# The routed experts of an encoder layer: results added to the residual in memory, per step

## The chip, the core and the metric

The kernel runs on one core of one Trainium2 chip. The metric is the device time of one execution in microseconds (us); three runs of the kernel before gave 1376.01, 1379.69 and 1382.04, median 1379.69. A core has a matrix engine (TensorE, PE in the profile, with its weight loads as PEld), VectorE (DVE), ScalarE (ACT), GpSimd (POOL) and SyncE (SP), each with an instruction stream of its own that runs in order, and 16 DMA engines that all of them feed. SP and POOL issue the transfers here. What SP issues goes over the hardware queue (q1 in the profile), what POOL issues over the software queue (q0).

## The reference

One encoder layer over 1296 positions (16 shared meta tokens, and two sequences of 1024 and 256): a mixer of windowed attention and a recurrence, then a mixture of 32 experts, then a final norm. The change lies in the expert part:

```python
def hier_moe(u, p):                       # u: [1280 tokens + meta, 1024], float32
    grp = argmax(u @ w_router_grp + b)    # one of 4 groups
    top_v, top_i = top_k(in_group_logits, 2)
    gates = softmax(top_v) * p_grp
    eid = grp * 8 + top_i                 # two experts for each token
    # for every expert e over its tokens xb, in blocks:
    #   hid = silu(xb @ w_g[e]) * (xb @ w_u[e]);  y = hid @ w_d[e]
    # out[token] += gate * y
h = h + hier_moe(rmsnorm(h), p)
return rmsnorm(h, ln_final_g)[:, N_META:]
```

An expert has three matrices of 512 x 1024 float32, 2 MB each. 1280 tokens go to two experts each, 2560 rows in all.

## The kernel before

The program has five stages that follow each other, each closed by a barrier of all engines: `project` and `keys` (projections, recurrence), `mix` (attention, output product, router), `plan`, `experts` and `combine`. For each block of 128 tokens, `mix` writes the residual to `h2_dram` and its norm to `u_dram`, and with two indirect DMAs the token numbers into `list_dram`, which has a list of 1280 places for every expert. `plan` reads the counts and makes with 27 small VectorE operations a table of steps: one step is up to 128 tokens of one expert. This input gives 35 steps over 32 experts.

`experts` (line 1681) does the steps. A float32 product is made of three products of rounded parts: every matrix and every activation is split into a high part (ACT copies it, rounding to the PE's format) and a low part (DVE subtracts). Weights come in chunks of 1 MB, 128 x 2048, six for an expert (two each of gate, up, down: G, U, D), into six slots `raw`, each with its `e_hi` and `e_lo`. A repeated expert's chunks are neither loaded nor split again.

- SP (`step`, lines 1789 to 1812) issues per step n one list (`ix`, 128 token numbers), and then the chunks D of step n, U of n+1 and G of n+2, each when DVE has done with the slot before. At the start it holds all but one chunk back until the first gather has landed.
- POOL (lines 1829 to 1868) gathers the 128 rows of `u_dram` that a list names into `ex` (two buffers; `gather(n + 3)` or so, two to three steps ahead), and stores the 128 x 1024 result of a step to consecutive rows of `y_dram` (`store`, L1847).
- PE (`step`, line 1914): turn x of step n+1 (8 transposes), up product of n (24 matmuls), first half of the gate product of n+1 (12), turn the hidden values of n (4 transposes), second half of that gate product (12), down product of n (24).
- ACT (`step`, line 1973): silu of n, high part of x of n+1, `y_from_psum` of the step before (L1970), and the high parts of six chunks with the high part of the hidden values among them. DVE makes the low parts and the product silu times up in the same order.
- At the start of `experts`, DVE computes for each token the rows of `y_dram` where its two results will stand (`slots`, lines 2053 to 2059).

`combine` (line 2075) then gathers, on POOL, 2 x 10 tiles of 128 rows from `y_dram` (L2115), adds each times its gate to the residual (L2142), norms and stores. Five of the ten residual tiles are loaded at the end of `experts`.

Of the kernel before, what the change touches and what calls it, by code (L numbers as in the profile page):

```python
# [69 lines left out]
FIELDS = 6  # L70
MAXPAIRS = (2 * REAL // P + EXP) // 2
YROWS = 2 * REAL + P
ROUT = 40

DEPTH = 5
# [28 lines left out]
def encoder(nc, a, out):  # L104
    top = ExitStack()
    with top:
# [6 lines left out]
        h2_dram = dram("h2_dram", [REAL, D], F32)  # L113
        u_dram = dram("u_dram", [REAL, D], F32)
        k_dram = dram("k_dram", [P, 2, 2, META + P + REAL + P], F32R)
        y_dram = dram("y_dram", [YROWS, D], F32)
        list_dram = dram("list_dram", [(EXP + 1) * LIST, 1], I32)
        table_dram = dram("table_dram", [MAXBLK, FIELDS], I32)

# [6 lines left out]
        expert1 = keep("expert1", [P, NB])  # L126
        expert2 = keep("expert2", [P, NB])
        place1 = keep("place1", [P, NB])
        place2 = keep("place2", [P, NB])
# [5 lines left out]
        with ExitStack() as mixer:  # L135
# [7 lines left out]
            with semaphores(nc) as own:  # L143
                project(nc, own, a, feat, k_pre, v_pre, ident, eps_t, iota_e, list_dram, y_dram)
# [11 lines left out]
                gate1, gate2, expert1, expert2, place1, place2, counts, h2_dram, u_dram, list_dram)  # L156
        slots = [top.enter_context(nc.sbuf_tensor(f"slot{j}", [P, NB], I32)) for j in range(2)]
        start = keep("start", [P, EXP])
        table = top.enter_context(nc.sbuf_tensor("table", [1, MAXBLK * FIELDS], I32))
        plan(nc, sem, counts, start, table, table_dram)  # L160

        z = [keep(f"z{s}", [P, D]) for s in range(DEPTH)]
        g_final = keep("g_final", [P, D])
        z_in = [sem(f"z_in{s}") for s in range(DEPTH)]
        g_in = sem("g_in")
        experts(nc, sem, a, ident, iota_e, start, expert1, expert2, place1, place2, slots, table, list_dram,
                u_dram, h2_dram, y_dram, g_final, z, g_in, z_in)
        combine(nc, sem, eps_t, gate1, gate2, slots, h2_dram, y_dram, out, g_final, z, g_in, z_in)


def project(nc, sem, a, feat, k_pre, v_pre, ident, eps_t, iota_e, list_dram, y_dram):
# [8 lines left out]
    with ExitStack() as ctx:  # L180
# [20 lines left out]
        zeros = a_g[:, 0:D]  # L201
        conv = h_g[:, :]
# [21 lines left out]
        fills = sem("fills")  # L224
        fill_dma = sem("fill_dma")
# [52 lines left out]
        def _(sp):  # L278
# [11 lines left out]
            for f in range(2):  # L290
# [3 lines left out]
            sp.wait_ge(fills, 2)  # L294
            sp.dma_start(list_dram.rearrange("(p c) o -> p (c o)", p=P),
                         zeros[:, 0:(EXP + 1) * LIST // P].bitcast(I32)).then_inc(fill_dma, 16)
            sp.dma_start(y_dram[2 * REAL:YROWS, :], zeros).then_inc(fill_dma, 16)
# [21 lines left out]
        @block.gpsimd  # L319
        def _(pool):  # L320
            pool.memset(zeros, 0.0).then_inc(fills, 1)
            pool.iota(iota_e[:, :], pattern=[[1, EXP]], base=0, channel_multiplier=0,
                      allow_small_or_imprecise_dtypes=True).then_inc(fills, 1)
            pool.memset(xr[:, :, :], 0.0).then_inc(xr_cleared, 1)

        @block.scalar
        def _(act):
# [86 lines left out]
            act.wait_ge(fill_dma, 32)  # L414
# [40 lines left out]
        def _(dve):  # L455
# [29 lines left out]

            dve.wait_ge(consts_in, 32)
# [322 lines left out]
def mix(nc, sem, a, spare, q_pre, rec, rstd_rec, w_hi, w_lo, k_dram, v_tok, v_meta, ident, eps_t, iota_e,  # L809
        gate1, gate2, expert1, expert2, place1, place2, counts, h2_dram, u_dram, list_dram):  # L810
# [6 lines left out]
    with ExitStack() as ctx:  # L817
# [68 lines left out]
        token_s = [sb(f"token_s{s}", [P, 1], I32) for s in range(RING)]  # L886
# [177 lines left out]
        def _(pool):  # L1064
# [41 lines left out]
            def place(b, s):  # L1106
# [4 lines left out]
                pool.tensor_copy(token_s[s][:, :], token[:, bass.ds(b, 1)]).then_inc(token_done, 1)  # L1111
                pool.wait_ge(token_done, b + 1)
                take_waits(pool)
                for j in range(2):
                    pool.indirect_dma_start(list_dram, bass.IndirectOffsetOnAxis(ap=addr[j][s][:, 0:1], axis=0),
                                            token_s[s][:, 0:1], None).then_inc(listed[s], 16)
# [461 lines left out]
PLAN_STEPS = 27  # L1578


def plan(nc, sem, counts, start, table, table_dram):

    with ExitStack() as ctx:
# [7 lines left out]
        count_end = sb("count_end", [P, EXP])  # L1597
# [5 lines left out]
        n_tokens = sb("n_tokens", [P, 1])  # L1603
        offset = sb("offset", [P, 1])
        row = sb("row", [P, FIELDS])
        row_i = sb("row_i", [P, FIELDS], I32)
        n_less_1 = sb("n_less_1", [P, 1])
        n_experts_1 = sb("n_experts_1", [P, 1])
        pairs_i = sb("pairs_i", [P, 1], I32)
# [8 lines left out]
        def _(pool):  # L1618
# [3 lines left out]
            pool.iota(n_less_1[:, :], pattern=[[0, 1]], base=-1, channel_multiplier=1,  # L1622
                      allow_small_or_imprecise_dtypes=True).then_inc(set_up, 1)

        @block.vector
        def _(dve):
# [8 lines left out]
            dve.wait_ge(set_up, 3)  # L1635
# [3 lines left out]
            then(dve.tensor_copy(blocks[:, :], blocks_i[:, :]))  # L1639
            then(dve.tensor_tensor_scan(block_end[:, :], ones[:, :], blocks[:, :], 0.0, ALU.mult, ALU.add))  # L1640
            then(dve.tensor_tensor_scan(count_end[:, :], ones[:, :], counts[:, :], 0.0, ALU.mult, ALU.add))
            then(dve.tensor_tensor(start[:, :], count_end[:, :], counts[:, :], ALU.subtract))
            then(dve.tensor_scalar(before_n[:, :], block_end[:, :], n_col[:, 0:1], None, ALU.is_le))
            then(dve.tensor_reduce(n_experts[:, :], before_n[:, :], AX.X, ALU.add))
            for total, each in ((n_blocks, blocks), (n_tokens, counts)):
                then(dve.tensor_tensor(weighed[:, :], before_n[:, :], each[:, :], ALU.mult))
                then(dve.tensor_reduce(total[:, :], weighed[:, :], AX.X, ALU.add))

            then(dve.tensor_tensor(offset[:, :], n_col[:, :], n_blocks[:, :], ALU.subtract))
            then(dve.tensor_scalar(offset[:, :], offset[:, :], float(P), None, ALU.mult))  # L1650
            then(dve.tensor_scalar(row[:, 0:1], n_experts[:, :], float(EXP - 1), None, ALU.min))

            then(dve.tensor_scalar(before_n[:, :], block_end[:, :], n_less_1[:, 0:1], None, ALU.is_le))
            then(dve.tensor_reduce(n_experts_1[:, :], before_n[:, :], AX.X, ALU.add))
            then(dve.scalar_tensor_tensor(out=n_experts_1[:, :], in0=n_less_1[:, :], scalar=0.0, in1=n_experts_1[:, :],
                                          op0=ALU.min, op1=ALU.add))
            then(dve.tensor_scalar(row[:, 3:4], n_experts_1[:, :], row[:, 0:1], None, ALU.is_lt))
            then(dve.scalar_tensor_tensor(out=row[:, 1:2], in0=n_experts[:, :], scalar=float(LIST), in1=offset[:, :],
                                          op0=ALU.mult, op1=ALU.add))
            then(dve.tensor_tensor(row[:, 2:3], n_tokens[:, :], offset[:, :], ALU.add))  # L1660

            then(dve.tensor_scalar(pairs_i[:, :], block_end[:, EXP - 1:EXP], -2.0, None, ALU.add))
            then(dve.tensor_single_scalar(pairs_i[:, :], pairs_i[:, :], 1, ALU.arith_shift_right))
            then(dve.tensor_copy(row_i[:, 0:4], row[:, 0:4]))
            then(dve.tensor_copy(row_i[:, 4:5], pairs_i[:, :]))
            then(dve.scalar_tensor_tensor(out=n_blocks[:, :], in0=pairs_i[:, :], scalar=-2.0, in1=block_end[:, EXP - 1:EXP],
                                          op0=ALU.mult, op1=ALU.add))
            then(dve.tensor_scalar(row_i[:, 5:6], n_blocks[:, :], -2.0, None, ALU.add))
# [10 lines left out]


def experts(nc, sem, a, ident, iota_e, start, expert1, expert2, place1, place2, slots, table, list_dram,
            u_dram, h2_dram, y_dram, g_final, z, g_in, z_in):

    with ExitStack() as ctx:
# [83 lines left out]
        def _(sp):  # L1775
# [11 lines left out]
            for m in range(2):  # L1787
                lists(m, m)
# [446 lines left out]
```

## Time and profile before

| what | value |
|---|---|
| runs | 1376.01, 1379.69, 1382.04 us |
| profiled execution | 1379.8 us, span of its instructions 1377.9 us |
| mean granted PE clock | 0.937 of full speed |
| PE busy | 1204.5 us (87%) |
| DVE, ACT, POOL busy | 921.3 (67%), 846.8 (61%), 196.7 (14%) us |
| HBM read, written | 274.21 MB, 37.96 MB |
| stages | to the plan 638 us, plan and start of the experts to 662 us (first gate product), steps to 1312 us, combine to the end |

The profiled execution took 1.9 us more than its span. Times in the rows count from the start of the span. A share of 1.00 of the DMA engines in a stretch means that the sum of the time of their packets was 16 times the stretch; packets of two queues can overlap in an engine, so it can pass 1. The matmuls overlap each other in the record: one follows the other after 0.23 us though each has 0.39.

### The profile page before, as it was taken

Reading aid. Unit: us, or ns where it says so; the run is one execution under the profiler, and the core shown is the slowest. Engines: PE = TensorE matmul, PEld = TensorE weight load, DVE = VectorE, ACT = ScalarE, POOL = GpSimd, SP = SyncE. Lnnn points to the kernel's source line nnn. Section 1 sums busy time; section 2 is a strip of 40 time slices with the busy share of each in tenths; the row PEclk is TensorE's granted clock in tenths of the full one; section 3 lists DMA queues with packets and bytes.
Section 4 is the critical chain, followed back from the end, with each engine's and each line's share of the span. In section 5 each row is a group of like instructions: output and inputs, shape, how many; then the busy total and the mean of one; then the engine's idle time right before and its main releaser. Section 6 shows DMA issues by size and latency. Waiting matters only on the chain. (4 is left out here: it accounts for less than half of the span.)

```text
span 1377.9 us, 22574 instructions
## 1 busy us (share of the span) xinstructions
PE 1204.5 (87%) x5971; PEld 1012.3 (73%) x5971; DVE 921.3 (67%) x1175; ACT 846.8 (61%) x1013; POOL 196.7 (14%) x201
## 2 busy tenths in 40 slices
PE   4999999847999999980799999999999999999900
PEld 3998888845788888860688888888888888888800
DVE  5575555244566766643788876665888888988638
ACT  6438888254666566630687765555777777778412
POOL 1000000031122322111011111101111011112041
PEclk9999999957999999985799999999999999999965
DMA  5210110093232343110999987678999999999758
GB/s 182 88 52 25 38 38 15 11 299 106 82 81 81 110 124 88 46 62 15 396 420 418 419 324 299 266 280 325 383 394 406 398 408 403 396 403 407 261 201 347
DMA packets 74905, 313.35 MB, mean 227 GB/s; under 512 B 15329, under 2 KB 26210, under 8 KB 50290
## 3 DMA queue, kind: packets, MB, share of 16 engines
q1 hardware_dynamic: 54450, 256.71, 48.5%
q0 software_dynamic: 20416, 56.18, 11.6%
q8 instruction: 17, 0.28, 0.1%
q14 instruction: 22, 0.18, 0.0%
HBM read 274.21 MB, written 37.96 MB: 227 GB/s over the span
## 5 line engine op out<-in xcount | busy, mean ns | idle before, releaser
L2011 DVE TENSOR_TENSOR e_lo<-raw,e_hi 128x2048 fp32r<-128x2048 f32 x192 | 432.5, 2287 | 68.8 <-ACT e_hi L1949 63.6
L1949 ACT ACTIVATE e_hi<-raw 128x2048 fp32r<-128x2048 f32 x192 | 356.1, 1912 | 59.3 <-DMA raw<-in_w_gate 39.7
L603 PE MATMUL pj<-h_hi,w_hi 128*128 128x432 f32 x336 | 123.5, 368 | 0.0
L1883 PE MATMUL ps_g<-e_hi,ex_hi 128*128 128x512 f32 x288 | 118.2, 410 | 4.1 <-DVE ex_lo L2026 4.1
L603 PE MATMUL pj<-h_lo,w_hi 128*128 128x432 f32 x336 | 121.0, 360 | 0.0
L603 PE MATMUL pj<-h_hi,w_lo 128*128 128x432 f32 x336 | 120.5, 358 | 0.0
L1883 PE MATMUL ps_g<-e_hi,ex_lo 128*128 128x512 f32 x288 | 115.0, 399 | 0.0
L1883 PE MATMUL ps_g<-e_lo,ex_hi 128*128 128x512 f32 x288 | 114.8, 399 | 0.0
L1883 PE MATMUL ps_u<-e_hi,ex_hi 128*128 128x512 f32 x280 | 113.8, 407 | 0.0
L1838 POOL DMA_INDIRECT ex<-u_dram,ix x37 | 67.9, 1836 | 319.3 <-DMA ix<-list_dram 318.9
L1883 PE MATMUL ps_u<-e_lo,ex_hi 128*128 128x512 f32 x280 | 110.8, 396 | 0.0
L1883 PE MATMUL ps_u<-e_hi,ex_lo 128*128 128x512 f32 x280 | 110.6, 395 | 0.0
L1908 PE MATMUL ps_ey<-e_hi,hid_lo 128*128 128x512 f32 x280 | 110.5, 395 | 0.0
L1908 PE MATMUL ps_ey<-e_hi,hid_hi 128*128 128x512 f32 x280 | 110.3, 394 | 0.0
L1908 PE MATMUL ps_ey<-e_lo,hid_hi 128*128 128x512 f32 x280 | 110.3, 394 | 0.0
L1965 ACT ACTIVATE ex_hi<-ps_ex 128x1024 fp32r<-128x1024 f32 x36 | 36.9, 1026 | 92.1 <-PE ps_ex L1875 92.1
L1410 DVE CUSTOM_DVE_ANT_0 probs<-ps_sc,mask,sink_bc 128x400 f32<-128x400 f32 x80 | 47.7, 631 | 41.8 <-PE ps_sc L1145 41.7
L1883 PEld LDWEIGHTS ps_g<-e_hi,ex_hi 128*128 128x128 f32 x288 | 55.1, 191 | 16.7 <-DVE ex_lo L2026 2.8
L1875 PE MATMUL ps_ex<-ident,ex 128*128 128x128 f32 x288 | 40.8, 286 | 30.2 <-DMA ex<-u_dram,ix 30.2
L603 PEld LDWEIGHTS pj<-h_hi,w_hi 128*128 128x128 f32 x336 | 63.5, 189 | 3.3
L603 PEld LDWEIGHTS pj<-h_lo,w_hi 128*128 128x128 f32 x336 | 63.7, 190 | 2.8
L603 PEld LDWEIGHTS pj<-h_hi,w_lo 128*128 128x128 f32 x336 | 63.5, 189 | 2.9
(276 smaller groups left out, 2354.8 us busy)
## 6 DMA issues: line engine op xcount, KB each, us to landing
raw<-in_w_gate SPq DMA_DIRECT2D x64, 1024.0 KB, 10.0
raw<-in_w_up SPq DMA_DIRECT2D x64, 1024.0 KB, 8.1
raw<-in_w_down SPq DMA_DIRECT2D x64, 1024.0 KB
y_dram<-y_sb POOLq DMA_DIRECT2D x35, 512.0 KB
k_win<-k_dram POOLq DMA_DIRECT2D x20, 384.0 KB, 7.3
w_raw<-in_w_in SPq DMA_DIRECT2D x14, 512.0 KB, 3.7
xh<-in_x SPq DMA_DIRECT2D x10, 512.0 KB, 6.5
h_dram<-xh SPq DMA_DIRECT2D x10, 512.0 KB, 2.8
```

Of the source, the lines that this page charges most:

```text
L603: mm = pe.matmul(ps[:, bank, 0:CH], w[s][:, k, :], h[:, k, cols], start=(k == 0 and n == 0), stop=(k == KD - 1 and n == 2))
L1410: dve.tensor_tensor_reduce(probs[:, h, :], ps_sc[h % 2][:, 0:KEYS], mask[s][:, :], HD ** -0.5, sink[:, h:h + 1], ALU.add, ALU.max, smax[:, ...
L1838: pool.indirect_dma_start(x[s][:, :], None, u_dram, bass.IndirectOffsetOnAxis(ap=ix[s][:, 0:1], axis=0)).then_inc(x_in[s], 16)
L1875: mm = pe.transpose(ps_x[:, c, k * P:(k + 1) * P], x[s][:, c * FE + k:(c + 1) * FE:KG], ident[:, :])
L1883: mm = pe.matmul(ps[:, :], xs[s][:, c * KG + k, :], w[slot][:, k * FE:(k + 1) * FE], start=(c == 0 and k == 0 and n == 0), stop=(c == 1 an ...
L1908: mm = pe.matmul(ps_y[:, i, :], h[:, c * KDN + k, :], w[D0 + c][:, k * D + i * BANK:k * D + (i + 1) * BANK], start=(c == 0 and k == 0 and ...
L1949: act.activation(w_hi[s][:, :], raw[s][:, :], ACT.Copy).then_inc(hi_done, 1)
L1965: act.activation(x_hi[s][:, :, :], square_x(ps_x), ACT.Copy).then_inc(x_hi_done, 1)
L2011: dve.tensor_tensor(w_lo[s][:, :], raw[s][:, :], w_hi[s][:, :].bitcast(F32), ALU.subtract).then_inc(lo_done, 1)
```

## The change

`combine` is gone. What it did is spread out:

- The lists. An entry of `list_dram` is now a pair, token number and gate. `mix` writes both (four small copies on POOL for a block of tokens in place of one). Unused entries name a row past the tokens, 1280 plus the entry's number modulo 128, so the 128 rows that a step names are all different; `h2_dram` and `u_dram` have 128 more rows for them, filled with zeros. Before, an unused entry named token 0.
- The plan has 18 operations in place of 27, gives every expert at least one step, and knows therefore that step 0 is expert 0. The slot operations at the start of `experts` are gone.
- The end of a step. ACT multiplies the result by the gates as it copies it out of PSUM, and POOL adds the tile to `h2_dram` with an indirect DMA that accumulates (`add_to_h2`, L1822 of the new file). Adds of two steps may name the same token, so the list of the next step's rows is only read, and `y_listed` only raised, when the add before has landed; `y_from_psum` waits for `y_listed`.
- The queues. POOL issues the two lists of a step (`ix_x` for the gather, `ix_y` for the add), SP only weights. x, its list and its split parts have one buffer in place of two. `gather(m)` is issued after x of step m-1 has been turned and, by POOL's order, after the list of y of step m-3 has landed.
- The order of PE: gate product of n+1, turn hidden of n, up of n+1, turn x of n+2, down of n. There is no gate product of a 36th step any more (before, the last step made one that nobody used).
- The start: both lists, then all six chunks of expert 0 and the final gain are issued at once. The end: after the last add has landed, the ten tiles of `h2_dram` are loaded, normed and stored.

The core of the diff:

```diff
-FIELDS = 6
+FIELDS = 4
@@ mix, POOL
-                pool.tensor_copy(token_s[s][:, :], token[:, bass.ds(b, 1)]).then_inc(token_done, 1)
+                for j, gate in enumerate((gate1, gate2)):
+                    pool.tensor_copy(entry[j][s][:, 0:1].bitcast(I32), token[:, bass.ds(b, 1)]).then_inc(token_done, 1)
+                    pool.tensor_copy(entry[j][s][:, 1:2], gate[:, bass.ds(b, 1)]).then_inc(token_done, 1)
...
@@ experts, SP
+            at = field(sp, 0, 1, EXP * LIST)
+            sp.dma_start(ix_x[:, :], list_dram[bass.ds(at, P), :]).then_inc(ix0_in, 16)
+            sp.dma_start(ix_y[:, :], list_dram[bass.ds(at, P), :]).then_inc(ix0_in, 16)
+            for weights, k, kind in ((a["w_gate"], KG, gates), (a["w_up"], KG, ups), (a["w_down"], KDN, downs)):
+                for c in range(2):
+                    src = weights[0].rearrange("(c p k) f -> c p (k f)", p=P, k=k)[c]
+                    sp.dma_start(kind[0][c][:, :], src).then_inc(kind[3][c], 16)
...
+            with sp.Fori(0, most) as i:
+                load_new(i + 3, a["w_gate"], KG, gates)
+                load_new(i + 3, a["w_up"], KG, ups)
+                load_new(i + 2, a["w_down"], KDN, downs)
+            sp.wait_ge(y_added, 16 * most + 32)
+            for b in range(NB):
+                sp.dma_start(z[b], h2_dram[b * P:(b + 1) * P, :]).then_inc(z_in[b], 16)
+            for b in range(NB):
+                sp.wait_ge(normed, b + 1)
+                sp.dma_start(out[b * P:(b + 1) * P, :], z[b]).then_inc(stored, 16)
...
@@ experts, POOL
+            def list_x(m):
+                pool.wait_ge(x_in, 16 * m)
+                list_of(m, ix_x, ix_x_in)
+            def list_y(m):
+                pool.wait_ge(y_added, 16 * m)
+                list_of(m, ix_y, ix_y_in)
+                pool.wait_ge(ix_y_in, 16 * m)
+                pool.sem_inc(y_listed, 1)
+            def gather(m):
+                    pool.wait_ge(ix_x_in, 16 * m)
+                    pool.wait_ge(x_turned, m)
+                pool.indirect_dma_start(x[:, :], None, u_dram, bass.IndirectOffsetOnAxis(ap=ix_x[:, 0:1], axis=0)
+            def add_to_h2(m):
+                pool.wait_ge(y_out, m + 2)
+                pool.indirect_dma_start(h2_dram, bass.IndirectOffsetOnAxis(ap=ix_y[:, 0:1], axis=0), y[:, :], None,
+                                        compute_op=ALU.add).then_inc(y_added, 16)
+            with pool.Fori(0, most) as i:
+                gather(i + 3)
+                add_to_h2(i)
+                list_x(i + 4)
+                list_y(i + 1)
...
@@ experts, PE
+            with pe.Fori(0, most + 1) as i:
+                gate(i + 1)
+                turn_hid(i)
+                up(i + 1)
+                turn_x(i + 2)
+                down(i)
+            turn_hid(most + 1)
+            down(most + 1)
...
@@ experts, ACT
+            def y_from_psum(m):
+                act.wait_ge(d_used, 2 * m + 2)
+                act.wait_ge(y_listed, m + 1)
+                act.activation(y[:, :], ps_y[:, :, :].rearrange("p b c -> p (b c)"), ACT.Copy,
+                               scale=ix_y[:, 1:2].bitcast(F32)).then_inc(y_out, 1)
...
+            with act.Fori(0, most + 1) as i:
+                silu_of(i + 1)
+                hid_split(i)
+                split_new(i + 2, gates)
+                x_split(i + 2)
+                split_new(i + 2, ups)
+                y_from_psum(i)
+                split_new(i + 1, downs)
+            hid_split(most + 1)
+            y_from_psum(most + 1)
```

Two places in the program's order, as each engine gets it. POOL, one step of the loop of `experts`, before (TENSOR_LOAD reads a field of the table; `ex` is x, `y_sb` the result):

```order
L1838 DMA ex<-u_dram,ix 128x1024
L1747 ISA
L1747 TENSOR_LOAD table
L1747 ISA x2
L1845 REGISTER_ALU
L1847 ISA
L1847 DMA y_dram<-y_sb 128x1024
```

And now (`h_dram` is `h2_dram`):

```order
L1816 DMA ex<-u_dram,ix_x 128x1024
L1820 REGISTER_ALU
L1822 DMA h_dram<-y_sb,ix_y 1408x1024
L1798 ISA
L1737 ISA
L1737 TENSOR_LOAD table
L1737 ISA x2
L1795 ISA
L1795 DMA ix_x<-list_dram 128x2
L1803 ISA
...
L1795 DMA ix_y<-list_dram 128x2
```

The store has become an add, and two reads of lists with their waits stand behind it, ahead of the next gather. (In the gap the rows of L1737 and L1795 stand once more.)

SP at the start of `experts`, before:

```order
L1782 DMA ix<-list_dram 128x1
...
L1778 DMA raw<-in_w_gate 128x2048
L1778 ISA
...
L1778 DMA raw<-in_w_up 128x2048 x2
```

And now:

```order
L1769 DMA raw_u<-in_w_up 128x2048 x2
L1769 DMA raw_d<-in_w_down 128x2048 x2
L1770 DMA g_final<-in_ln_final_g 128x1024
L1737 TENSOR_LOAD table
...
L1758 COMPARE_AND_BRANCH
L1750 ISA
L1750 DMA raw_g<-in_w_gate 128x2048
```

Six chunks (the two of the gate matrix stand ahead of these rows) are in the queue ahead of anything that waits, where one was before; the wait for the first gather stood ahead of the second chunk.

## Rows read from the trace of the kernel before

**Rows 1.** The page's slices of the span: granted PE clock and DMA share

```profile
PEclk9999999957999999985799999999999999999965
DMA  5210110093232343110999987678999999999758
```

**Rows 2.** Stretches: us, busy by engine (instructions), PE clock, DMA share, GB/s

```profile
694.00:712.00 18.00, 18.00 (x85) 14.75 (x84) 16.16 (x10) 14.26 (x11) 2.09 (x2) 1.00 1.02 420
803.00:821.00 18.00, 18.00 (x84) 14.76 (x84) 11.64 (x8) 10.21 (x9) 1.54 (x2) 1.00 0.66 241
949.00:967.00 18.00, 18.00 (x85) 14.76 (x84) 11.30 (x7) 10.21 (x9) 1.54 (x2) 1.00 0.97 366
1000.00:1100.00 100.00, 100.00 (x463) 82.03 (x462) 86.65 (x50) 75.94 (x56) 12.92 (x11) 1.00 1.00 400
1312.00:1378.00 66.00, 0.00 (x0) 0.00 (x0) 39.79 (x40) 16.67 (x32) 20.86 (x21) 0.54 0.73 286
```

**Rows 3.** Timeline of ACT, copies of a step's result: start us, us

```profile
693.82 1.03 ACT L1970 ACTIVATE y_sb<-ps_ey 128x1024 f32<-128x1024 f32 x1
1149.56 1.02 ACT L1970 ACTIVATE y_sb<-ps_ey 128x1024 f32<-128x1024 f32 x1
1167.80 1.02 ACT L1970 ACTIVATE y_sb<-ps_ey 128x1024 f32<-128x1024 f32 x1
1311.93 1.02 ACT L1970 ACTIVATE y_sb<-ps_ey 128x1024 f32<-128x1024 f32 x1 [7.89 <-PE ps_ey L1908]
```

**Rows 4.** The gathers of x over all steps (the tile's own view)

```profile
L1838 POOL DMA_INDIRECT ex<-u_dram,ix x37: 954/1819/3032, 651.8 to 1284.5; - x37
DMA to landing us min/median/max: 5.2/9.1/11.7
```

**Rows 5.** DMA view of 930 to 980: KB each, median us to landing

```profile
q1 hardware_dynamic: 2419, 14.54, 75.4%
q0 software_dynamic: 720, 2.62, 13.3%
ix<-list_dram SPq DMA_DIRECT2D x3, 0.5 KB, 6.4
ex<-u_dram,ix POOLq DMA_INDIRECT x3, 6.5
```

**Rows 6.** The same view of 1030 to 1080

```profile
ex<-u_dram,ix POOLq DMA_INDIRECT x3, 10.2
ix<-list_dram SPq DMA_DIRECT2D x3, 0.5 KB, 9.1
```

**Rows 7.** Timeline of POOL: the row after a result's copy

```profile
1151.43 0.57 POOL L1847 DMA_DIRECT2D y_dram<-y_sb  x1 [7.56 <-ACT y_sb L1970]
```

**Rows 8.** The lists over all steps (the tile's own view)

```profile
DMA to landing us min/median/max: 2.0/9.1/12.3
```

**Rows 9.** The plan's first and last operation of 27, timeline of DVE

```profile
638.08 0.18 DVE L1637 TENSOR_SCALAR blocks_i<-counts 128x32 int32<-128x32 f32 x1 [8.29 <-POOL n_less L1622]
643.73 0.15 DVE L1668 TENSOR_SCALAR row_i<-n_blocks 128x1 int32<-128x1 f32 x1
```

**Rows 10.** Timeline at the start of the experts

```profile
651.70 6.62 SPq L1778 DMA_DIRECT2D raw<-in_w_gate  x2
651.78 1.00 POOL L1838 DMA_INDIRECT ex<-u_dram,ix  x1 [13.73 <-DMA ix<-list_dram]
...
656.57 1.91 ACT L1949 ACTIVATE e_hi<-raw 128x2048 fp32r<-128x2048 f32 x1 [31.97 <-DMA raw<-in_w_gate]
657.87 1.98 PE L1875 MATMUL ps_ex<-ident,ex 128*128 128x128 f32 x8 [30.24 <-DMA ex<-u_dram,ix]
...
662.23 0.79 PE L1883 MATMUL ps_g<-e_hi,ex_hi 128*128 128x512 f32 x1 [2.37 <-DVE ex_lo L2026]
```

**Rows 11.** The page's groups: split of a chunk, on DVE and on ACT

```profile
L2011 DVE TENSOR_TENSOR e_lo<-raw,e_hi 128x2048 fp32r<-128x2048 f32 x192 | 432.5, 2287 | 68.8 <-ACT e_hi L1949 63.6
L1949 ACT ACTIVATE e_hi<-raw 128x2048 fp32r<-128x2048 f32 x192 | 356.1, 1912 | 59.3 <-DMA raw<-in_w_gate 39.7
```

**Rows 12.** Timeline of the end

```profile
1336.89 1.06 ACT L2123 ACTIVATE c_square<-z 128x1024 f32<-128x1024 f32 x1 [1.13 <-DVE z L2142]
...
1338.07 0.29 ACT L2125 ACTIVATE c_rms<-c_ssq,eps_t 128x1 f32<-128x1 f32 x1
...
1373.56 1.28 DVE L2134 SCALAR_TENSOR_TENSOR cz<-cz,c_rstd,g_final 128x1024 f32<-128x1024 f32 x1
```

More of the change, by code:

```diff
@@ L1653, in _ @@
[L1653 to L1657, printed above, removed]
+            then(dve.tensor_tensor(offset[:, :], offset[:, :], real[:, :], ALU.mult))
@@ L1665, in _ @@
[L1665 to L1668, printed above, removed]
+            then(dve.tensor_scalar(row[:, 3:4], block_end[:, EXP - 1:EXP], -2.0, None, ALU.add))
+            then(dve.tensor_copy(row_i[:, :], row[:, :]))
@@ L1678, in _, with experts @@
             sp.wait_ge(table_in, 16)
-def experts(nc, sem, a, ident, iota_e, start, expert1, expert2, place1, place2, slots, table, list_dram,
-            u_dram, h2_dram, y_dram, g_final, z, g_in, z_in):
+def experts(nc, sem, a, ident, eps_t, table, list_dram, u_dram, h2_dram, out):
     with ExitStack() as ctx:
@@ new lines, in load, with load_new @@
+                sp.dma_start(raw[c][:, :], src).then_inc(arrived[c], 16)
+            def load_new(m, weights, k, kind):
+                e, new = field(sp, m, 0, EXP - 1), is_new(sp, m)
+                lo_done, arrived = kind[5], kind[3]
+                for c in range(2):
+                    sp.wait_ge(lo_done, 2 * m - 1 + c)
+                    sp.sem_inc(waited_sp, 1)
+                    with sp.If(new > 0):
+                        load(weights, k, e, c, kind)
+                    with sp.If(new < 1):
+                        sp.sem_inc(arrived[c], 16)
@@ L1841, in store @@
-            def store(n):
-                at = field(pool, n, 2, 2 * REAL)
-                pool.wait_ge(y_out, n + 2)
-                pool.wait_ge(y_stored, 16 * n) if not isinstance(n, int) or n > 0 else None
-                pool.sem_inc(waited, 1)
-                pool.dma_start(y_dram[bass.ds(at, P), :], y[:, :]).then_inc(y_stored, 16)
-            for m in range(3):
-                gather(m, m % 2)
-            gather(3, 1)
-            store(0)
-            more = more_pairs(pool)
-            with pool.Fori(0, more) as i:
-                gather(2 * i + 4, 0)
-                store(2 * i + 1)
-                gather(2 * i + 5, 1)
-                store(2 * i + 2)
@@ new lines, in add_to_h2 @@
+            def add_to_h2(m):
+                pool.wait_ge(y_out, m + 2)
+                pool.sem_inc(waited, 1)
+                pool.indirect_dma_start(h2_dram, bass.IndirectOffsetOnAxis(ap=ix_y[:, 0:1], axis=0), y[:, :], None,
+                                        compute_op=ALU.add).then_inc(y_added, 16)
+            gather(0)
+            pool.sem_inc(y_listed, 1)
+            for m in range(1, 3):
+                list_x(m)
+                gather(m)
+            list_x(3)
+            most = blocks_less_2(pool)
@@ L1987, in _ @@
-            for s in range(SLOTS):
-                split(s, s, 0)
-                if s == 0:
-                    x_split(0, 0)
-            step(0, 0, None)
-            step(1, 1, 0)
-            more = more_pairs(act)
-            with act.Fori(0, more) as i:
-                step(2 * i + 2, 0, 2 * i + 1)
-                step(2 * i + 3, 1, 2 * i + 2)
-            odd = one_more(act)
-            with act.If(odd > 0):
-                step(2 * more + 2, 0, 2 * more + 1)
-            y_from_psum(2 * more + 1 + odd)
```

559 lines of the change are left out of this document (231 added, 328 removed).

## The prediction

> **What bounds the kernel now.** I read the slices first, then stretches of one step, then the timeline of one engine. From slice 20 on PE is at full clock and the DMA share stands at 9 [rows 1]. The experts are one rhythm: in a stretch of a step PE is busy for all of it whatever the load of the others [rows 2], and a result is copied every 18.24 us (1167.80 less 1149.56), from 693.82 to 1311.93 with 34 periods of 18.18 on the mean [rows 3]. So PE sets the steps. But the DMA engines are hardly behind it: in 1000 to 1100 they are at 1.00 of their time with 400 GB/s, and the most that they gave in any stretch of a step is 420 [rows 2]. A step with a new expert moves 6.29 MB of weights, 0.52 MB of x and 0.52 MB of y, 7.34 MB; at 420 GB/s that takes 17.5 us. There is 4% of slack. Where an expert repeats the share falls to 0.66 [rows 2]; 3 of 35 steps are repeats. After the steps come 66 us in which PE does nothing [rows 2]; this is the part that the change goes at.
>
> **Plan and lists.** 27 operations take 643.73 + 0.15 - 638.08 = 5.8 us, 0.215 each [rows 9]. Nine fewer: -1.9. Three more small copies on POOL ahead of the last list writes, at about the same price each: +0.7. Those of other blocks lie beside the attention. The slot operations ran while the first transfers were out and bring nothing. The new fills at the very start are bounded by 0 and 2 us; POOL and DVE wait for data there, and I take 0. Sum -1.2.
>
> **Start of the experts.** Before, the first gather, issued at 651.78 with one chunk beside it, was in at 657.87, 6.1 us [rows 10]. Now six chunks are ahead of it in the other queue, and it takes what a gather takes under load, 9.1 [rows 4] to 10.2 [rows 6]: +3.3. Turning x, splitting it and the gate product follow as before. Then x of step 1 is turned only after the up product of step 0, and with one buffer for the parts nothing covers turning and splitting it (1.1, 1.0, 1.2 us and hand-offs): PE stands some 4.6 us in place of 2.1, +2.5. Bounds of both together: 3 and 10.
>
> **Work that goes.** The unused gate product is 24 matmuls. They follow each other at 0.23 us, -5.6. The order of the rest leaves the sum of PE's work as it is, 72 matmuls and 12 transposes a step.
>
> **Last step.** The ACT order puts `y_from_psum(33)` (1.0) and two chunk splits ahead of the hidden split of step 34. After down(33) ends, that is 1.1 + 3.8 on ACT, then the rest of DVE's two splits of 2.29 and its part of the hidden split [rows 11], about 8.4 us until down(34) may start, 0.7 of it work: +7.7. Bounds 3 and 9 (3 if DVE keeps up with ACT from the first chunk).
>
> These give the end of the last down product without any new wait in the loop: 1311.7 - 1.2 + 3.3 + 2.5 - 5.6 + 7.7 = 1318.4.
>
> **The end.** 1.1 for the copy; 0.5 and an add without load. A gather without load lands in 5.2 [rows 4]; the add reads its target as well, which I price as a second pass of 0.52 MB, 1.25 us at 420 GB/s: 7.0. Then the first tile lands after about 3.2, and ACT norms one in about 1.6 (square at 1336.89, its root done at 1338.36, and the hand-off) [rows 12], ten in 16, with a table load of 1.3; the ten loads, 12.5 us of data, hide below. DVE closes the last tile in 1.5, and from there to the end it is 3.1 as now (1374.84 to 1377.9) [rows 12]. 1318.4 + 1.1 + 7.0 + 3.2 + 17.3 + 1.5 + 3.1 = 1351.6 for the span, against 1377.9: -26.3.
>
> **The loop, where the question lies.** A new ring is closed over POOL: list of y in, gather issued, add issued, add landed, field of the table read, list of y read, `y_listed`, copy of y, next add. POOL's order puts the gather ahead of the add, in the same queue, so the add's data come behind the gather's. Everything in the ring is DMA latency, and none of it was in a ring before. Under the load of full steps: gather to its landing 10.2 [rows 6]; the add behind it 5.0 (two passes of 1.25, each interleaved with as much weight traffic); 0.9 from one POOL event to the next issue, as from the end of the copy at 1150.58 to the store at 1151.43 [rows 3, 7]; the list 6, between 2.0 without load [rows 8] and 9.1 behind weights on SP's queue [rows 6]; hand-offs 0.6. Together 22.7 us, more than 18.24. At the lighter load of 930 to 980, where the two queues use 75.4% and 13.3% [rows 5], the same sum is 6.5 (gather) + 3.5 (add) + 0.9 + 5.0 (list, 6.4 on SP) + 0.6 = 16.5. So the ring's time hangs on the load, and the load on the period: a step now moves 7.86 MB with the add's second pass, 18.7 us at 420 GB/s. Between share 0.89 (16.5) and 1.00 (22.7) a line has the slope 56 us for 1; the share 18.7 / period meets it at 19.8 (share 0.945; 16.5 + 56 x 0.055 = 19.6). I take 19.8, 1.6 above PE's time.
> How many steps pay: a repeat drops gate and up chunks in one step and down chunks in the next, so six steps are light, and the last two have no loads: 34 periods - 8 = 26. 26 x 1.6 = 41. A late copy of y holds PE up only after some 4.5 us of lag (ACT has that until the parts it owes PE are late), once in each of the two full stretches: -9. The loop costs +32. Bounds: 0, if the ring stays under 18.24, and +80, if the add takes four passes: 8.9 MB, 21.2 us a step, 3 x 26.
>
> By the fit that the Trainium skill gives for transfers issued from GpSimd (DMA: Bandwidth & Descriptors, Anatomy of one DMA — SWDGE (gpsimd) path: about 2.0 us and bytes at 436 GB/s), gather, add and list would be some 3.2, 3.2 and 2.0 us, the ring would close in about 10 us, and the loop term would be 0; the gathers here took 9.1 on the median and never under 5.2 [rows 4], so this trace doesn't bear it out under load. The same page (SDMA does more than copy) calls the DMA's add an elementwise reduction of two streams; by that the add has two passes, no run here shows it yet.
>
> **Sum.** Span 1351.6 + 32 = 1383.6, and 1.9 around it as in the profiled execution, 1379.8 over a span of 1377.9: 1385.5. The profiled execution lies 0.1 from the median of the runs, so this stands against 1379.7: the end is worth 26 us and the ring takes it back.
>
> **Rivals.**
> 1. *The ring stays hidden.* The chunk loads are issued by three pairs that lie more evenly in a step than before, so a queue is less often full, and the short transfers may land as in 930 to 980, ring 16.5 [rows 5]. Then PE's 18.24 stands, except for 18.7 of data in full steps, which the 14 us that a chunk may take mostly absorb (a slot is filled once in 18.24, and its two splits take 4.2 [rows 11]). 1353.5 to 1370; I put it at 1360. Against it: POOL's serial order, and the 10.2 of rows 6. The Trainium skill's fit named above would give this case as well.
> 2. *The add is slow.* Read, add and write of a row may not stream as copies do. If it takes four passes, the DMA engines need 21.2 us a step: 1353.5 + 77 = 1430. The price decides from two passes on, where the DMA engines' 18.7 pass PE's 18.24; below it there is no loss from this cause. No row shows an adding transfer, so nothing speaks against it but that plain ones run at 420 GB/s [rows 2]. This is the case on the slower side.
>
> **How the numbers follow.** My case 0.42, with a range of its own from 1372 (period 19.3) to 1402 (20.4); rival 1, 0.33, 1353 to 1372; rival 2, 0.25, 1402 to 1460. A change under 0.5% (6.9 us) can't be told from none here. Faster than 1372.8: rival 1 and an edge of my case, 0.37. Within: a little under half of my case, 0.20. Slower than 1386.6: 0.43. For the range I leave out a tenth at each side: 1352 to 1430.
>
> **What would show it.** Period of the copies of y in full steps: 19.8 (mine), 18.2 to 18.7 (rival 1), over 20.5 (rival 2), and 18.2 in the light steps in all. ACT's copy should wait for POOL's list of y, 1 to 3 us in full steps. The first gate product at 664 to 666, the last copy 27 to 35 us from the end. The add should land 5 to 7 us after issue at the end and 12 or more in the loop; DMA share about 0.94 to 1.0. I am wrong if PE never waits in the loop, or if what it waits for is a chunk or x and not the ring.

## The result, and the profile after

The changed kernel takes 1402.05 us on the median of four runs (1397.08 to 1406.29), the kernel before 1378.83 beside it: ratio 1.0154, 95% interval 1.0123 to 1.0185, slower by 1.5%. The profiled execution is the longest of the four: 1406.3 us, span 1404.7. All numbers from the trace are those of that one execution.

The slices of the page after, PE clock and DMA share, against [rows 1]:

```profile
PEclk9999999955999999985899999999999999999985
DMA  6211010192222342113999978879999999999938
```

The DMA engines are at 9 from slice 28 on, as before, though 10.3 MB less are moved. Stretches of the kernel after (columns as in [rows 2]):

```profile
860.00:950.00 90.00, 89.38 (x408) 72.49 (x407) 59.59 (x37) 51.66 (x40) 20.50 (x20) 1.00 0.83 275
1000.00:1100.00 100.00, 96.15 (x427) 78.25 (x426) 80.96 (x47) 72.04 (x54) 20.49 (x21) 0.97 1.00 365
1100.00:1200.00 100.00, 93.27 (x414) 74.28 (x413) 75.88 (x44) 66.53 (x48) 19.54 (x20) 0.98 1.01 371
```

PE now has holes in the full steps, and some of its busy time is at a lower granted clock. The DMA engines are full at 365 GB/s where they gave 400 [rows 2]. The copies of y run from 707.82 to 1367.41, a mean period of 19.4 against 18.18, and no longer evenly: between 975.99 and 1317.22 the mean of 17 periods is 20.07, in turns of about 23 and 17. What holds the copy up stands in two views, the copy's line in the page's groups, and what ACT and PE waited for in 700 to 1320:

```profile
L1961 ACT ACTIVATE y_sb<-ps_ey,ix_y 128x1024 f32<-128x1024 f32 x35 | 39.1, 1117 | 149.0 <-POOLq L1807 124.0
```

```profile
ACT y_sb L1961 <- POOLq L1807: 116.3, 29, 7.0
PE ps_ex L1856 <- DMA ex<-u_dram,ix_x: 20.0, 12, 4.1
```

L1807 is the raising of `y_listed`. The copy waits for POOL's list in 29 steps, 4.0 us each on the mean; x, now in one buffer, is late for PE in 12. The ring itself, timeline of POOL:

```profile
1016.60 1.64 POOL L1822 DMA_INDIRECT h_dram<-y_sb,ix_y  x1 [0.30 <-issue]
1026.55 0.58 POOL L1795 DMA_DIRECT2D ix_x<-list_dram  x1 [8.32 <-issue]
1031.55 0.56 POOL L1795 DMA_DIRECT2D ix_y<-list_dram  x1 [4.42 <-issue]
1037.78 1.00 POOL L1816 DMA_INDIRECT ex<-u_dram,ix_x  x1 [5.66 <-ACT y_sb L1961]
1039.08 1.63 POOL L1822 DMA_INDIRECT h_dram<-y_sb,ix_y  x1 [0.30 <-issue]
1045.08 0.58 POOL L1795 DMA_DIRECT2D ix_x<-list_dram  x1 [4.37 <-issue]
1047.73 0.56 POOL L1795 DMA_DIRECT2D ix_y<-list_dram  x1 [2.07 <-issue]
1054.64 1.45 POOL L1816 DMA_INDIRECT ex<-u_dram,ix_x  x1 [6.36 <-issue]
1056.40 1.65 POOL L1822 DMA_INDIRECT h_dram<-y_sb,ix_y  x1 [0.30 <-issue]
```

and ACT inside it:

```profile
1036.62 1.12 ACT L1961 ACTIVATE y_sb<-ps_ey,ix_y 128x1024 f32<-128x1024 f32 x1 [4.97 <-POOLq L1807]
```

Read it from add to add. The add is issued at 1016.60; its data are in when POOL may issue the next list, 1031.55 (15.0); the list is in and `y_listed` raised at 1036.6 (5.1); POOL needs 1.2 to the gather, the copy of 1.12 fits beside it, and 1.3 to the add: 22.5 us. The next turn is 8.7 (1039.08 to 1047.73), 5.8 to ACT's copy at 1053.50, 1.1 and 1.8: 17.3. Nothing in either is work of PE, and the mean, 19.9, is the period. The two turns differ in the load that the transfers meet. The queue of the weights, in 1017 to 1031 (first) and in 1039 to 1048:

```profile
q1 hardware_dynamic: 547, 3.97, 71.5%
```

```profile
q1 hardware_dynamic: 208, 1.51, 45.8%
```

The DMA engines are full in both (a share of 1.01 and 0.99), but the add shares them with much less weight traffic in the second, and lands in 8.7 in place of 15.0. A reading that fits, and that no run here tests: after a long turn PE, ACT and DVE are late, slots come free late, and the add meets few weight loads; it lands soon, the engines catch up and ask for weights in a bunch, and the next turn is long again.

The start, against [rows 10], and the end:

```profile
644.18 0.18 DVE L1624 TENSOR_SCALAR blocks_i<-counts 128x32 int32<-128x32 f32 x1 [7.96 <-POOL n_col L1609]
647.78 0.17 DVE L1645 CAST row_i<-row 128x4 int32<-128x4 f32 x1
...
656.26 0.99 POOL L1816 DMA_INDIRECT ex<-u_dram,ix_x  x1 [12.12 <-DMA ix_y<-list_dram]
665.36 1.98 PE L1856 MATMUL ps_ex<-ident,ex 128*128 128x128 f32 x8 [31.32 <-DMA ex<-u_dram,ix_x]
669.71 0.80 PE L1865 MATMUL ps_g<-g_hi,ex_hi 128*128 128x512 f32 x1 [2.37 <-DVE ex_lo L2013]
```

```profile
1367.41 1.11 ACT L1961 ACTIVATE y_sb<-ps_ey,ix_y 128x1024 f32<-128x1024 f32 x1 [10.49 <-PE ps_ey L1902]
1369.35 1.61 POOL L1822 DMA_INDIRECT h_dram<-y_sb,ix_y  x1 [7.68 <-ACT y_sb L1961]
1375.82 1.76 SPq L1785 DMA_DIRECT2D raw_g<-h_dram  x4
1379.06 1.06 ACT L1987 ACTIVATE ex<-raw_g 128x1024 f32<-128x1024 f32 x1 [10.53 <-DMA raw_g<-h_dram]
...
1394.57 1.73 SPq L1788 DMA_DIRECT2D out<-raw_d  x2
1394.65 1.28 DVE L2052 SCALAR_TENSOR_TENSOR raw_d<-raw_d,c_rstd,g_final 128x1024 f32<-128x1024 f32 x1
```

The end is 37.3 us from the last copy, against 66.0 before. The last norm ends at 1395.9, and 8.8 us more pass until the last store has landed.

### The profile page after: what moved, and what is told of

Read it like the earlier page. It is cut to its first block and busy times, and to the rows that moved or that the text cites. A ratio compares the mean times of both kernels' runs of the same rounds, so it can differ in the third digit from the quotient of the medians.

```text
span 1404.7 us, 22170 instructions
## 1 busy us (share of the span) xinstructions
PE 1224.9 (87%) x5947; PEld 1021.6 (73%) x5947; DVE 886.9 (63%) x1138; ACT 844.0 (60%) x1013; POOL 251.0 (18%) x280
## 5 line engine op out<-in xcount | busy, mean ns | idle before, releaser
L1997 DVE TENSOR_TENSOR d_lo<-raw_d,d_hi 128x2048 fp32r<-128x2048 f32 x64 | 143.8, 2288 | 121.8 <-ACT d_hi L1929 121.8
L1997 DVE TENSOR_TENSOR g_lo<-raw_g,g_hi 128x2048 fp32r<-128x2048 f32 x64 | 143.7, 2285 | 27.3 <-ACT g_hi L1929 27.3
L1997 DVE TENSOR_TENSOR u_lo<-raw_u,u_hi 128x2048 fp32r<-128x2048 f32 x64 | 143.7, 2286 | 8.5 <-ACT u_hi L1929 8.1
L1929 ACT ACTIVATE g_hi<-raw_g 128x2048 fp32r<-128x2048 f32 x64 | 119.2, 1916 | 31.7 <-DMA raw_g<-in_w_gate 29.1
L1902 PE MATMUL ps_ey<-d_hi,hid_hi 128*128 128x512 f32 x280 | 116.8, 417 | 12.5 <-DVE hid_lo L2026 12.4
L1865 PE MATMUL ps_g<-g_hi,ex_hi 128*128 128x512 f32 x280 | 113.3, 405 | 7.5 <-DVE ex_lo L2013 7.5
L1929 ACT ACTIVATE u_hi<-raw_u 128x2048 fp32r<-128x2048 f32 x64 | 118.9, 1913 | 0.0
L1929 ACT ACTIVATE d_hi<-raw_d 128x2048 fp32r<-128x2048 f32 x64 | 118.6, 1904 | 0.0
L1865 PE MATMUL ps_u<-u_hi,ex_hi 128*128 128x512 f32 x280 | 113.4, 405 | 0.0
L1902 PE MATMUL ps_ey<-d_lo,hid_hi 128*128 128x512 f32 x280 | 113.3, 405 | 0.0
```

The costliest lines, as they stand in the source:

```text
L1865: mm = pe.matmul(ps[:, :], xs[:, c * KG + k, :], w[c][:, k * FE:(k + 1) * FE], start=(c == 0 and k == 0 and j == 0), stop=(c == 1 and k == ...
L1902: mm = pe.matmul(ps_y[:, i, :], h[:, c * KDN + k, :], w[c][:, cols], start=(c == 0 and k == 0 and j == 0), stop=(c == 1 and k == KDN - 1 a ...
L1929: act.activation(hi[c][:, :], raw[c][:, :], ACT.Copy).then_inc(hi_done, 1)
L1997: dve.tensor_tensor(lo[c][:, :], raw[c][:, :], hi[c][:, :].bitcast(F32), ALU.subtract).then_inc(lo_done, 1)
```

## The experiments

Each kernel is the changed kernel with one edit, the last two are the version with the list ahead with one more. "Periods" are those of the copies of y. Ratios stand to runs of the kernel before on the same chip (medians 1377.75 to 1379.7 us); copies are from the profiled executions. The theory: the ring over POOL sets the period in full steps. The rivals: the adds' DMA time does, or the weights' load, or x in its one buffer.

| kernel | us, median (lowest to highest) | ratio to before, 95% | first, last copy of y | their distance |
|---|---|---|---|---|
| before | 1378.83 | 1 | 693.82, 1311.93 | 618.1 |
| after | 1402.05 (1397.08 to 1406.29) | 1.0154 (1.0123 to 1.0185) | 707.82, 1367.41 | 659.6 |
| list ahead | 1361.56 (1361.02 to 1369.42) | 0.9888 (0.9854 to 0.9922) | 700.60, 1321.36 | 620.8 |
| plain scatter | 1374.92 (1369.0 to 1378.65) | 0.9968 (0.9952 to 0.9984) | 702.38, 1334.89 | 632.5 |
| half the weights | 1365.38 (1363.78 to 1366.98) | 0.9899 (0.9876 to 0.9921) | 708.86, 1327.62 | 618.8 |
| add first | 1507.28 (1503.68 to 1508.79) | 1.0925 (1.0901 to 1.0948) | 703.57, 1465.42 | 761.9 |
| list twice | 1513.56 (1508.44 to 1518.67) | 1.0971 (1.0901 to 1.1042) | 700.23, 1468.88 | 768.7 |
| list ahead, again | 1361.53 (1359.41 to 1365.37) | 0.9872 (0.9828 to 0.9916) | 699.52, 1322.66 | 623.1 |
| list ahead, chunks held | 1365.65 (1361.92 to 1375.68) | 0.991 (0.9883 to 0.9936) | 707.20, 1329.76 | 622.6 |
| list ahead, plain scatter | 1358.34 (1355.63 to 1363.89) | 0.986 (0.9813 to 0.9906) | 699.46, 1318.84 | 619.4 |

**The list read ahead.** The list of y goes into a tile of its own while the adds are out, and is only copied when the add before has landed; the order that two adds on one token need is kept.

```diff
-            def list_y(m):
+            def take_y(m):
+                pool.wait_ge(ix_y_in, 16 * m)
                 pool.wait_ge(y_added, 16 * m)
...
-                list_of(m, ix_y, ix_y_in)
-                pool.wait_ge(ix_y_in, 16 * m)
-                pool.sem_inc(y_listed, 1)
+                pool.tensor_copy(ix_y[:, :], ix_n[:, :]).then_inc(y_listed, 1)
+                pool.wait_ge(y_listed, m + 1)
...
+            list_of(1, ix_n, ix_y_in)
...
-                list_y(i + 1)
+                take_y(i + 1)
+                list_of(i + 2, ix_n, ix_y_in)
```

> The changed kernel with the next step's list for the add fetched early into a tile of its own and copied (a 128x2 copy on GpSimd) once the add before has landed, so that the list's DMA (landing 6.0 us on the median) and the table read ahead of it (0.9) leave the ring. Theory, the ring of gather, add and list sets full steps at 20.1 us: the ring falls to about 13 us, and the steps fall to what the DMA engines need, 14.8 us of weight packets, 1.3 of gather and 3.0 of add, 19.1 us: 26 x 1.0 less, 1376. Rival, the DMA engines' throughput alone set 20.1 (their share is 1.00 in 1000 to 1200): the list's few bytes change nothing, 1402 within 5. Rival, the one buffer of x does it: PE waits for the gather as before, no change either, 1402.

Measured: 40.5 us less than after, 14 below the 1376 expected, and 1.1% under the kernel before. (The 6.0 us in the expectation is the median of a view that mixes the lists with the adds that use them; the 70 lists alone took 5.3 on the median.) 25 periods of 18.27 follow each other, then seven of 18.6 to 18.8. In its timeline only one copy stands between the add's landing and `y_listed`:

```profile
1042.63 0.34 POOL L1807 COPY ix_y<-ix_n 128x2 int32<-128x2 int32 x1 [3.08 <-DMA h_dram<-y_sb,ix_y]
1044.37 0.56 POOL L1796 DMA_DIRECT2D ix_n<-list_dram  x1 [1.40 <-issue]
1045.53 2.69 POOL L1818 DMA_INDIRECT ex<-u_dram,ix_x  x1 [0.61 <-issue]
1049.79 1.63 POOL L1824 DMA_INDIRECT h_dram<-y_sb,ix_y  x1 [1.57 <-ACT y_sb L1965]
```

```profile
1000.00:1100.00 100.00, 100.00 (x462) 82.15 (x461) 86.45 (x52) 77.58 (x55) 30.03 (x27) 1.00 1.02 388
```

PE is busy throughout in this stretch, 1000 to 1100, at a DMA share even above that of after, so neither the throughput of the DMA engines nor x in its one buffer set the longer periods. PE waits for x only once from 690 to 1330:

```profile
PE ps_ex L1860 <- DMA ex<-u_dram,ix_x: 0.5, 1, 0.5
```

One transfer of 1 KB out of the ring, with the read of the table ahead of it, took nearly all of its cost away; I had expected a part of it. The reason is in the last row of POOL above: the add waits for ACT's copy again, so the ring is open, and gather and add may take what they take.

**A plain scatter in place of the add.** `compute_op=ALU.add` removed: rows are overwritten, the sum over the experts is left out.

```diff
-                                        compute_op=ALU.add).then_inc(y_added, 16)
+                                        ).then_inc(y_added, 16)
```

> The changed kernel with the indirect DMA of a step's result writing its rows in place of adding them (the sum over experts is left out of the computation; order and waits are unchanged). It prices the add. Its packets of 4 KB should take 0.16 us like the gather's, against about 0.37 for the add's. Ring theory: the ring gets about 3.5 us shorter (8 packets an engine, interleaved with weights), full steps at 18.3 to 18.8: 1360 to 1370. Throughput theory: a step's DMA time falls from 19.1 to 17.4 us, under PE's 18.24: full steps at 18.24, 1354. If the add costs nothing beyond a write: 1402.

Measured: 27 us less than after, and 5 us above the band that the ring theory expected: the 17 periods that have a mean of 20.07 in after have 19.2 here, not 18.3 to 18.8. The waits of 700 to 1320:

```profile
ACT y_sb L1961 <- POOLq L1807: 72.9, 22, 8.1
```

The ring is shorter but still closed. The queues' share of the span prices the add, software queue of after, of this kernel:

```profile
q0 software_dynamic: 19632, 45.26, 13.6%
```

```profile
q0 software_dynamic: 19632, 45.26, 9.9%
```

Same packets, same bytes: 0.136 x 1404.7 - 0.099 x 1371.0 = 55 us over 35 adds, 1.6 us each of all 16 engines. (This is an estimate: it takes the gathers and lists, which share that queue, as equal in both.) Alone at the end, in 12 us around the add and 10 us around the plain scatter, the software queue took, of after and of this kernel,

```profile
q0 software_dynamic: 144, 0.52, 28.7%
```

```profile
q0 software_dynamic: 144, 0.52, 12.9%
```

3.44 us against 1.29, so an add costs 2.7 plain passes there, and lands in 6.4 against 3.4. The Trainium skill's fit for transfers issued from GpSimd (DMA: Bandwidth & Descriptors, Anatomy of one DMA — SWDGE (gpsimd) path) gives, as an estimate, 3.2 us for 0.52 MB. The trace agrees for this plain transfer on idle engines, 3.4, and not under load: over all steps this scatter took 8.9 on the median.

**Half of the weights.** After the first steps each chunk loads half of its columns (the results are those of stale weights).

```diff
-                sp.dma_start(raw[c][:, :], src).then_inc(arrived[c], 16)
+                sp.dma_start(raw[c][:, 0:CHUNK // 2], src[:, 0:CHUNK // 2]).then_inc(arrived[c], 16)
```

> The changed kernel with every weight load after the first expert's cut to its first half (half of each chunk's data is left out of the computation, splits and products stay whole). It tests whether the ring's time hangs on the load of the DMA engines. If it does: gather, add and list land in about 5, 5 and 2 to 3 us, the ring is under 16 and hides, full steps at PE's 18.24, 1354. If the ring's time were fixed latency: full steps stay at 20 us, 1402.

Measured: a stretch of full steps, and what the copy of y waited for over all steps (us, times):

```profile
1000.00:1100.00 100.00, 100.00 (x461) 81.98 (x460) 86.37 (x50) 77.02 (x56) 28.24 (x22) 1.00 0.77 226
```

```profile
  PE ps_ey L1902: 46.8, 26
  POOLq L1807: 13.3, 8
```

At a share of 0.77 the same ring stays under PE's period: 618.8 us from first copy to last, as before the change. The ring's time is made of what its transfers meet, as the prediction had it. The time is 11 above the 1354 expected. Some 7 of these lie in the expectation, which took 26 x 1.83 = 48 us off where the loop gave 40.8 (659.6 to 618.8). The rest may lie ahead of the experts: the plan began at 645.7 in this execution, as late as in after (644.2), and at 636.6 in that with the list ahead; PE's clock in 328 to 344 was granted at 0.50 in the first two and 0.89 in the third.

**The add ahead of the gather.** POOL's order alone:

```diff
-                gather(i + 3)
                 add_to_h2(i)
+                gather(i + 3)
```

> The changed kernel with GpSimd's order turned in the loop: the add of step i ahead of the gather of step i+3. Ring theory: the add no longer stands behind a gather of 128 rows, the ring gets 3 to 5 us shorter, but x arrives later by the wait for y; full steps between 18.6 and 20, 1365 to 1400. Rival, x's one buffer sets the steps: PE waits longer for x, full steps at 21 or more, 1425 and up.

Measured: 105 us slower than after. The band of the ring theory missed, and the rival came, x's one buffer. The add does not wait behind the gather now, but the gather waits for the copy of y behind which the add stands, and PE waited for x 86.5 us in 24 steps, where it was 20.0 in 12 (timelines of POOL and of PE):

```profile
1038.05 1.68 POOL L1822 DMA_INDIRECT h_dram<-y_sb,ix_y  x1 [7.33 <-ACT y_sb L1961]
1040.03 2.14 POOL L1816 DMA_INDIRECT ex<-u_dram,ix_x  x1 [0.30 <-issue]
...
1061.10 1.68 POOL L1822 DMA_INDIRECT h_dram<-y_sb,ix_y  x1 [7.07 <-ACT y_sb L1961]
```

```profile
1050.69 1.23 PE L1856 MATMUL ps_ex<-ident,ex 128*128 128x128 f32 x8 [3.01 <-DMA ex<-u_dram,ix_x]
```

A second ring, through PE: gather 10.7, turning x and the down product, a part of it at a lowered clock, 8.4 until the copy starts, the copy and its hand-off 2.0, from the add to the next gather 2.0: 23.05, from add to add. The order of the changed kernel is the better one. The copy's wait for POOL's list fell from 116.3 to 21.3 us, so the first ring hardly binds here; what it would do without the second can't be read.

**The list read twice,** one read after the other, before `y_listed`:

```diff
                 list_of(m, ix_y, ix_y_in)
-                pool.wait_ge(ix_y_in, 16 * m)
+                pool.wait_ge(ix_y_in, 32 * m - 16)
+                pool.sem_inc(waited, 1)
+                list_of(m, ix_y, ix_y_in)
+                pool.wait_ge(ix_y_in, 32 * m)
```

> The changed kernel with the list of y read twice, one read after the other, before y_listed is raised. If the ring over POOL (gather, add, landing, list, copy) sets the period in full steps, a second read adds its whole latency there, 5 to 6 us a step of 20.1, less what PE's slack of both orders takes up: periods of about 25 in full steps and 20 in light ones, in all 1402 + 26 x 5.3 + some for the light ones = 1530 to 1580. If the longer periods come from DMA time or the clock and the list only stands beside them, the added transfer of 1 KB costs nothing: 1402 to 1412.

The timeline of POOL, one turn:

```profile
1039.65 1.64 POOL L1825 DMA_INDIRECT h_dram<-y_sb,ix_y  x1 [0.30 <-issue]
1045.00 0.58 POOL L1795 DMA_DIRECT2D ix_x<-list_dram  x1 [3.71 <-issue]
1047.40 0.56 POOL L1795 DMA_DIRECT2D ix_y<-list_dram  x1 [1.82 <-issue]
1054.27 0.54 POOL L1795 DMA_DIRECT2D ix_y<-list_dram  x1 [6.30 <-issue]
1060.87 1.02 POOL L1819 DMA_INDIRECT ex<-u_dram,ix_x  x1 [6.07 <-issue]
```

34 KB more of transfers cost 111 us, 3.2 a step: the DMA time of a list of 1 KB can't do that, its landing in a ring can. It is less than the 5.3 expected for each full step, and the time is 16 below the band of 1530 to 1580. The read itself takes 5 to 7 a turn, but with it the ring meets less load: the share in 1000 to 1100 fell from 1.00 to 0.89, and the add landed in 7.0 on the median in place of 10.1.

**Three on top of the list ahead,** on one chip: the version itself again; with SyncE holding five of the six first chunks until the first gather has landed (the diff below); and with the plain scatter as above.

```diff
+                        if kind is gates and c == 0:
+                            sp.wait_ge(x_in, 16)
```

> The version with the list of y read ahead once more, as the partner on the same chip for the two versions built on it: 1361 to 1363 expected, ratio to the kernel before 0.985 to 0.992.

> The version with the list read ahead, and at the start of the experts SyncE holds five of the six first chunks back until the first gather has landed. If the queueing of the first gather behind 6 MB of weights costs what the trace shows (9.1 us in place of 6.1), the gather lands in about 6, the first gate product comes some 3 us after the plan's lists sooner, and the time falls by up to 3 us against the version with the list ahead (1361.6: 1358 to 1359). The rival: the held chunks are then late themselves (the up and down chunks are needed 9 and 18 us after the gate product begins, six chunks need 15 us), PE waits for the up product's weights and nothing or less than nothing is won: 1361 to 1364.

> The version with the list read ahead, with the add turned into a plain scatter (the sum over experts is left out). It prices the add once the ring no longer sets the period. Theory: with the list off the ring the add costs only DMA time, about 1.6 us of all engines a step, which shows where the DMA engines are full: the steps from 26 on, 18.6 to 18.8 with the add, return to 18.24; 4 to 5 us over 8 to 10 steps, and the end is shorter by at most 1: 1355 to 1358. Rival: the add is for nothing once the ring is open and the longer periods at the end come from the weights alone: 1360 to 1362. If it falls by over 10 us the ring was still closed in part by the add.

The repeat gives the same time. With the chunks held, the gather landed in 4.3 us (651.85 to 656.20) where it took 9.2 in the repeat and 9.1 in the first such execution. But the second gate chunk was split 12.1 us after the first list was issued, in place of 8.8 and 8.5, and since the parts of x are made behind it on ACT and DVE, the gate product began after 17.5 in place of 16.7 and 16.5; the up product came after 25.5 in place of 24.8 and 23.6, the first copy of y after 58.4 in place of 57.2 and 54.6. So queueing the first gather behind 6 MB costs it 5 us, and holding the chunks back wins nothing of them. The medians lie 4.1 us apart, above even the rival's 1361 to 1364, but the intervals of the two ratios overlap: that holding is slower isn't shown.

With the plain scatter all full periods are 18.3 to the end. The medians are 3.2 us apart, which the intervals don't tell from none; first to last copy is 3.8 shorter than in the repeat and 1.4 than in the first. Stretches 1200 to 1300 of the version with the list ahead (first) and of that with the plain scatter:

```profile
1200.00:1300.00 100.00, 99.19 (x456) 80.51 (x455) 83.48 (x48) 72.66 (x53) 35.06 (x28) 1.00 1.01 378
```

```profile
1200.00:1300.00 100.00, 100.00 (x463) 82.13 (x462) 81.93 (x49) 71.68 (x51) 26.37 (x28) 1.00 0.91 358
```

So with the ring open an add costs DMA time alone, 0.5 us a step (18.8 less 18.3), and only where the lead of the weights is used up: a chunk takes 13.9 to 14.1 us to land there, 7.5 to 9.1 with the scatter.

## Why the forecast held, and where it was off

The time forecast was 1385, the result 1402, inside the range and at the upper edge of my own case. The range says little by itself: 1352 to 1430 had room for a faster kernel, an equal one and a slower one, and 1402 is also where the case of the slow add began. That the kernel is slower for the reason given is what the runs bear out, and they tell the two cases apart. By the terms, spans 1383.6 and 1404.7:

| term | forecast | measured | difference |
|---|---|---|---|
| first operation of the plan | 638.1, as before | 644.2 | +6.1 |
| from there to the first copy of y, more than before's 55.7 | +10.2 (-1.2 +3.3 +2.5, and 5.6 for `up(1)`, which stands ahead of it now) | +7.9 | -2.3 |
| first to last copy | 646.4 | 659.6 | +13.2 |
| last copy to the end | 33.2 | 37.3 | +4.1 |

- **Before the plan.** PE's clock was granted at 0.50 in 328 to 344 after, and at 0.92 before. The versions with the list ahead and with the list read twice, with the same `mix`, began their plans at 636.6 and 636.1 with 0.89 and 0.97 there, and that with half the weights at 645.7 with 0.50. In all ten profiled executions 0.50 stands only in these two, and the other eight began their plans at 633.5 to 639.9. So it varies between executions of the same code and isn't the change's; a part of the 4 us by which this execution is above the median may be here.
- **Plan and start.** The plan's operations take 647.95 - 644.18 = 3.8 where they took 5.8 [rows 9]. The gather took 9.1, as read from [rows 4]: +3.0 for 3.3. Held: the first gate product came 25.5 us after the plan's first operation, 24.2 before.
- **The loop**, the term that decided. Mechanism and place as forecast: `y_listed` held by gather, add, landing and list in POOL's order. Taking one link away removes 38.8 us (659.6 to 620.8), doubling it adds 109, and lowering the load hides it. Its size was mis-stated: +32 forecast, +42.0 measured (the 33 periods ahead of the last take 643.9, at 18.24 they would take 601.9). The part that was off is the credit in "the loop costs +32": I gave back 9 us for ACT's slack of 4.5, once in each full stretch. No such credit shows: the ring lags from the first full step on (periods 21.4, 16.1, 23.1), and the 26 full periods have a mean of 19.96 for the 19.8 of the load line, so that 26 x 1.6 = 41.6 without the credit was nearly right. How near the period came is in part luck: it is a mean of turns of about 17 and 23, which the sum did not foresee. Of the 42.0 the version without the ring still has 2.7, almost all of it in its seven periods of 18.6 to 18.8. The 1.7 of the last step stands below; 1.5 of the 13.2 is left over between the two countings.
- **The add.** Two passes were taken, four were the rival. It is 2.7 passes alone and some 1.6 us more than a plain one under load, and full steps with the ring open take 18.8, against the 18.7 that two passes gave. So the slow add, the second rival, can't be what sets 20.07. The first rival, short transfers that land early so that the ring hides, came only when the weights were halved.
- **The last step.** Copy 33 to 34 took 15.7 in place of 14.0 (5.6 + 0.7 + 7.7).
- **The end.** The add landed in 6.4 and the first tile 3.2 after its load was issued, as forecast; the norms took 1.37 us a tile in place of 1.6. What I left out is the stores: reads and writes of ten tiles, 10.5 MB, share the DMA engines, the last two stores took 8.2 us to land, and 8.8 passed from the last norm to the end where I had 3.1.
- **What PE waits for.** I named x as what would prove me wrong. It did wait for x, 20.0 us in 12 steps; with the list ahead, x still in one buffer, 0.5 us are left, so these waits followed from the ring: the gather is issued only after the list of y.

What stays open: how the 38.8 us of the ring divide between the copy's and x's lateness, why PE's clock fell before the plan in two of these executions, and why the periods alternate rather than settle at 19.9. The changing load in the two turns is seen, that it keeps the alternation up is only argued.

The version with the list of y read ahead beats both kernels: 1361.5 us, 1.1 to 1.3% under the kernel before (intervals above), 2.9% under the changed one by the medians (these two were not run side by side). There the end's 27 us are kept (38.8 us from the last copy, 66.0 before), and nothing is paid for them in the loop but 2.7.

## What to carry to other kernels

When a step of a serial stream waits for its own transfer's landing, add up the whole circle of landings at the load that the stream meets, and compare it with the step; how small a transfer in it is doesn't matter. What need not wait for the landing (here: fetching the list) is fetched ahead, and only its use is ordered. Before reordering or holding transfers back, look who waits for the ones that move: the add ahead of the gather lost 105 us here, and holding the first chunks back won nothing.

## What the runs showed of the hardware

- An indirect DMA that accumulates in memory: 3.44 us of all engines for 0.52 MB against 1.29 for a plain one, landing 6.4 against 3.4 when alone; 10.1 on the median over all steps (6.0 to 14.0).
- A list of 1 KB landed in 1.7 us at the start, ahead of the weights, and in 5.3 on the median of the 70 lists that POOL issued, 7.8 at most.
- In stretches of 100 us at a DMA share of 1.00 to 1.02 the engines gave 400 to 402 GB/s in the kernel before and 400 to 404 with the list ahead and the plain scatter, and 361 to 393 with adds among them. The adds are not all of it: the kernel with the plain scatter and the ring gave 389 at 1.00.
